# Attention: the new rows' projection with high and low parts in one 40-column stationary

## The chip, the cores and the metric

The kernel runs on one core of a Trainium2 chip. The metric is the device time of one execution in microseconds (us). The core has five engines that run their own instruction streams in order and meet through semaphores: TensorE (PE in the profile, PEld for its weight loads), VectorE (DVE), ScalarE (ACT), GpSimd (POOL) and SyncE (SP), which issues most DMAs.

## The reference

Two layers of a decoder are computed for 1024 prompt rows and 8 new ("sample") rows that share every weight. The change touches layer 0's attention, and in it the projection of the 8 new rows:

```
def attn_project(x, w_qkv):
    qkv = x @ w_qkv                      # x: 8 x 1024, w_qkv: 1024 x 1536
    q, k, v = split into 16 q heads, 4 k heads, 4 v heads of 64

def swa_sample(x, k_buf, v_buf, w_qkv, sinks, w_o):
    q, k, v = attn_project(x, w_qkv)
    q, k = rope(q, pos), rope(k, pos)    # rotary positions
    o = sink_attention(q, cache + k, cache + v)
    return o @ w_o, ...
```

All arrays are float32. The kernel multiplies in the format fp32r and splits every operand into a high and a low part (x = xh + xl, w = wh + wl, low = value - high); a product is the sum of xh*wh, xh*wl and xl*wh.

## The kernel before, in words

Attention comes first (the first 390 us), in four groups of heads, `attention(g)`, once on each engine. A group has its own weights `wh`, `wl`: three slabs for q and k and v (384 output columns in all) and two for the output projection. The rows go through in nine blocks: b = 0 to 7 are 128 prompt rows each, b = 8 (`NB`) is the 8 new rows.

On TensorE, `project(b)` multiplies a block: for each of 8 contraction tiles of 128, three products (`accumulate`, L677 to L679), each with the rows as the stationary operand (128 columns, or 8 for b = 8) and 384 weight columns as the moving one. The result stands in bank 0 or 1 (b % 2). Then a pipeline of steps follows, a few blocks behind: `scores` (L810), `turn` (transposes of q and k, L785, for the new rows L788), `values` (L831), `turn_probs` (L821), and `down`, the output projection (L677 to L679 again, on `a_oh` and `a_ol`). The order is written out by hand. In a turn t of the loop `for t in range(NB + 1)` TensorE runs project(t), scores(t - 2), turn(t - 1), values(t - 4), turn_probs(t - 3). After the loop, in groups 0 to 2, it runs turn(8) and then `down(0, 4)`; in the last group `down(4, 6)` stands in turn 8 before values, and `down(6, 8)` before turn(8). TensorE's `down` of q = 4 in the last group waits for the rotary products of the new rows, since it writes the bank that these read.

Behind project(8) the data go like this. ScalarE copies the values out of the bank (`v_in`, L1361, `a_vs`). VectorE waits for that copy (semaphore `v_fp`), and makes the rotary products (`rope`, L1918 to L1920, `a_t`). GpSimd adds them up (`add_rope`, L2616 and L2621, `a_qk`), and TensorE turns the sum (L788). VectorE's order in a turn t is `inverse(t - 3)` (L1959, L1961), `rope(t)`, `shift(t - 2)` (mask, maximum and sink, L1946 to L1954), `t_lo(t - 1)` (low parts of the turned q and k, L1926 and L1928), `heads_lo(t - 4)` (L1967). TensorE's turn(b) waits for `a_qk` of block b and for t_lo(b - 1), since it overwrites the bank that t_lo reads. GpSimd also multiplies the probabilities by the inverse sums (`probs`, L2627).

The steps of `scores`, `shift`, `t_hi` and `t_lo` run over prompt blocks only, apart from t_lo(8), a copy (L1933).

Of the kernel before, what the change touches and what calls it, by code (L numbers as in the profile page):

```python
# [6 lines left out]
F32 = mybir.dt.float32  # L7
F32R = mybir.dt.float32r
ALU = mybir.AluOpType
# [3 lines left out]
P = 128  # L13
D = 1024
SEQ = 1024
NS = 8
TOK = SEQ + NS
KT = D // P
# [6 lines left out]
NB = SEQ // W  # L25
# [104 lines left out]
J = {key: n + 1 for n, key in enumerate(JOBS)}  # L130
# [229 lines left out]
def fillers():  # L360
# [10 lines left out]
    for n in range(NB):  # L371
# [13 lines left out]
        "p_in prod rot plain out_r0 out_r1 out_p0 out_p1").split()  # L385
ATT_SEMS = ("table_in turn_in cache_in rope_t v_in v_fp qk back t_hi t_lo score shifted small small2 expd "
            "inv probs pt pt_in heads heads_hi heads_lo kv_out win_out s_sc s_scc "
            "s_tr s_mx s_ex s_p s_pt s_ptc s_o s_of s_oh s_ol dchain").split()
RET_SEMS = ("m_in dec_in cq0 cq1 cv cg0 cg1 turned q_hi q_lo v_hi v_lo k_hi k_lo inner inn i_hi i_lo kv state out_ "
            "s_hi s_lo stats small root ga back ob ob_hi ob_lo oh_out ol_out st_in0 st_in1 st_out0 st_out1 decay outer "  # L390
            "x_in x_ing masks rows x_part x_sum xv xv_out vb x_o x_stats x_small x_root x_ga x_back xo xo_hi xo_lo xoh_out xol_out "
# [3 lines left out]
def after(eng, sem, value):  # L395

    if value > 0:
        eng.wait_ge(sem, value)
# [39 lines left out]
def build(nc, A):  # L438
    ctx = ExitStack()
    with ctx:  # L440
        K = Kit()
# [8 lines left out]
        def place(at):  # L450

            here = [at]

            def sb(name, shape, dt=F32):
                size = 4 * math.prod(shape[1:])
                t = nc.alloc_sbuf_tensor_at(name, shape, dt, offset=here[0], align_bytes=32)
                here[0] += (size + 31) // 32 * 32
                assert here[0] <= TOP, (name, here[0])
                return t
            return sb  # L460

        sb = place(BASE)
# [16 lines left out]
        sb = place(REGION)  # L479
# [10 lines left out]
        sb = place(at_t2 + 32 * TH)  # L490
        K.t2r = sb("x_t2r", [P, 2, 4, TH])
        sb = place(at_t2 + 80 * TH)
        K.t1r = sb("x_t1r", [P, 4, TH])
        sb = place(at_t2)
        K.ha = (sb("h_ah", [P, 4, TOK], F32R), sb("h_al", [P, 4, TOK], F32R))
        K.h0 = (sb("h_0h", [P, BATCH, TOK], F32R), sb("h_0l", [P, BATCH, TOK], F32R))
        sb = place(REGION + 49568)
        K.ms = sb("n_ms", [P, CH])
        K.sq = sb("n_sq", [P, KT, CH])
        sb = place(REGION)  # L500
        K.lsq = sb("n_lsq", [P, KT, CH])
        sb = place(REGION)
        K.hs = sb("h_in", [P, 2, 4, CH])
        at_x = BASE + 4 * SLAB * (RAW + 12)
        sb = place(at_x + 4 * KT * TOK)
        K.xr = sb("x_r", [P, 4, TOK])
        sb = place(at_x)
# [4 lines left out]
        for i in range(2):  # L512
            sb = place(BASE + 4 * SLAB * (RAW + 6 * i + 4))
# [3 lines left out]
        sb = place(REGION)  # L517
# [23 lines left out]
        K.same = sb("same", [32, NS])  # L541
        K.a_t1 = sb("a_t1", [P, 2, 320])
        K.a_t2 = sb("a_t2", [P, 2, 320])
        sb("a_gap", [P, 1536])
        K.a_sm = sb("a_sm", [P, GH, 2 * W])
        K.a_qh = sb("a_qh", [P, 256], F32R)
        K.a_ql = sb("a_ql", [P, 256], F32R)
# [5 lines left out]
        sb = place(REGION)  # L553
# [36 lines left out]
        sb = place(BASE + 4 * SLAB * (RAW + 4))  # L590
# [3 lines left out]
        sb = place(BASE + 4 * SLAB * (RAW + 6 + 4))  # L594
# [31 lines left out]
def wait_slab(eng, S, s):  # L626

    wait_unit(eng, S, UNIT_OF_SLAB[s])
# [54 lines left out]
def tensor_engine(pe, K):  # L683
    S, T, R, bank = K.S, K.T, K.R, K.bank
    wh, wl, xh, xl, ident = K.wh, K.wl, K.xh, K.xl, K.ident
# [61 lines left out]
    def attention(g):  # L747
# [8 lines left out]
        def project(b):  # L756
            m = P if b < NB else NS
            if b == 0:
                wait_slab(pe, S, 5 * g + 2)
            if b < 2 and g:  # L760
                pe.wait_ge(*freed(g, b))
            if g == 0:
                pe.wait_ge(S["x_lo"], 1 + sum((b + 1) * W > end for _, end in PIECES[:-1]))
            if b >= 2:
                pe.wait_ge(T["rope_t"], (NB + 1) * g + b - 1)
            if last and b == NB:
                pe.wait_ge(S["yadd"], 24 * g + 3)
            o = bank[b % 2][0:m, 0:384].rearrange("m (a n) -> m a n", a=3)
            t = slice(b * W, b * W + m)
            terms = []  # L770
            for k in range(KT):
                kk = slice(k * P, (k + 1) * P)
                terms.append((xh[:, k, t], xl[:, k, t], wh[:, 0:3, kk], wl[:, 0:3, kk]))
            accumulate(pe, o, terms).then_inc(S["jobs"], 1)
# [473 lines left out]
def scalar_engine(act, K):  # L1248
    A, S, T, R, bank = K.A, K.S, K.T, K.R, K.bank
    xh, y = K.xh, K.y  # L1250
# [97 lines left out]
    def attention(g):  # L1348
        last = g == NG - 1

        def v_in(b):
            act.wait_ge(S["jobs"], J["qkv", g, b])
            if b < NB:
                after(act, T["heads"], NB * g + max(b - 4, 0))
                act.activation(K.a_v[:, b % VR, :], bank[b % 2][:, 320:384], ACT.Copy).then_inc(T["v_in"], 1)
            if b == NB - 1:
                after(act, T["kv_out"], 64 * g)
                act.activation(K.a_vf[:, :], bank[b % 2][:, 320:384], ACT.Copy).then_inc(T["v_fp"], 1)
            if b == NB:
                after(act, T["s_o"], g)  # L1360
                act.activation(K.a_vs[:, :], bank[b % 2][0:NS, 320:384], ACT.Copy).then_inc(T["v_fp"], 1)  # L1361

        def t_hi(b):
# [451 lines left out]
def vector_engine(dve, K):  # L1815
    S, T, R, bank = K.S, K.T, K.R, K.bank
    xh, xl, y, ident = K.xh, K.xl, K.y, K.ident
    split = [0]

    def split_lo(n):  # L1820

        dve.wait_ge(S["hi_done"], n + 1)
        source, (hi, lo) = unit_source(K, n), unit_hi_lo(K, n)
        if n >= U_LAST:
            i = n - U_LAST
            dve.scalar_tensor_tensor(lo, source, K.wm[:, i:i + 1], hi.bitcast(F32), ALU.add, ALU.subtract).then_inc(S["lo_done"], 1)
            return
        dve.tensor_tensor(lo, source, hi.bitcast(F32), ALU.subtract).then_inc(S["lo_done"], 1)  # L1828
# [74 lines left out]
    def attention(g):  # L1903
        last = g == NG - 1

        def rope(b):
            m = P if b < NB else NS
            if b < NB:
                dve.wait_ge(T["v_in"], NB * g + b + 1)
            if b >= NB - 1:  # L1910
                dve.wait_ge(T["v_fp"], 2 * g + b - NB + 2)
            after(dve, T["qk"], 2 * (NB + 1) * g + (2 * (b - 1) if b >= 2 else 0))
            src = bank[b % 2][0:m, 0:320].rearrange("m (h a n) -> m h a n", h=5, a=2)
            a1 = K.a_t1[0:m, b % 2, :].rearrange("m (h a n) -> m h a n", h=5, a=2)
            a2 = K.a_t2[0:m, b % 2, :].rearrange("m (h a n) -> m h a n", h=5, a=2)
            cs = K.cosT[0:m, b:b + 1, :].rearrange("m (a c) n -> m a c n", a=1)
            sn = K.sinT[0:m, b, :].rearrange("m (a n) -> m a n", a=1)
            dve.tensor_tensor(a1, src, cs.to_broadcast([m, 5, 2, 32]), ALU.mult)  # L1918
            dve.tensor_tensor(a2[:, :, 1, :], src[:, :, 0, :], sn.to_broadcast([m, 5, 32]), ALU.mult)
            dve.scalar_tensor_tensor(a2[:, :, 0, :], src[:, :, 1, :], -1.0, sn.to_broadcast([m, 5, 32]),  # L1920
                                     ALU.mult, ALU.mult).then_inc(T["rope_t"], 1)
# [101 lines left out]
        def add_y(q0, q1):  # L2023
            for q in range(q0, q1):
                add(("ao", g, q))

        for t in range(NB + 1):
            if t >= 3:
                inverse(t - 3)
            rope(t)  # L2030
            if t >= 2:
                shift(t - 2)
            if t >= 1:
                t_lo(t - 1)
            if g == 0 and t < 2:
                x_lo(2 + t)
            if g == 0 and t in (4, 5):
                split_lo(t - 1)
            if last and t == NB:
                add_y(4, 6)  # L2040
            if t >= 4:
                heads_lo(t - 4)
            if last and t == NB - 1:
                add_y(0, 4)
# [1156 lines left out]
```

## Time and profile before

| | us |
|---|---|
| median of 3 runs | 2746.16 |
| shortest and longest run | 2745.92 and 2748.1 |
| the profiled execution: its span, first to last instruction | 2744.9 |
| TensorE busy in it | 2692.8 |
| VectorE busy in it | 1638.9 |
| ScalarE busy in it | 1036.3 |

Of the profiled execution only its span is given; the median of the runs lies 1.3 us above it, for what lies before the first and after the last instruction and the spread of the runs. TensorE is busy in 98% of the span, so most of the time is its products one after another; where it waits shows in its timeline as idle time, with the instruction that ended the wait.

### The profile page before, as it was taken

To read this page: it belongs to the slowest core of one execution; us is meant where nothing else is said; L and a number is where in the kernel's file an instruction comes from. 1 tells how busy PE (TensorE), PEld (TensorE's weight loads), DVE (VectorE), ACT (ScalarE), POOL (GpSimd) and SP (SyncE) were. 2 spreads that over 40 slices of the span, in tenths; PEclk is the share of its full clock that TensorE was granted. 3 is DMA by queue.
4 is the path that set the end of the run, shared out by engine and by line. 5 is a ranking of instruction groups with operands and counts; after the bars stand their busy time and mean duration, and the time that the engine had idled before them with its cause. 6 is when DMAs were issued, how large, how long until landed. Compare 5 with 4: busy or idle time off the path is not lost.

```text
span 2744.9 us, 47495 instructions
## 1 busy us (share of the span) xinstructions
PE 2692.8 (98%) x19166; PEld 2587.3 (94%) x19166; DVE 1638.9 (60%) x3042; ACT 1036.3 (38%) x1930; POOL 673.5 (25%) x534
## 2 busy tenths in 40 slices
PE   8999989999999999999999999999999999999997
PEld 7888879999999999999999999999999999999997
DVE  6556578676767445615446354366688666766455
ACT  5445455433343112323343433432254344332123
POOL 2344351322220002403213122111241223220021
PEclk9999999999999999999999999999999999999999
DMA  4210111222224232235666565686512222223321
GB/s 141 82 44 15 40 33 55 70 86 78 86 78 154 74 112 68 79 111 166 184 197 189 184 194 186 204 267 215 171 55 73 79 84 71 86 96 123 114 73 62
DMA packets 218665, 307.27 MB, mean 112 GB/s; under 512 B 30608, under 2 KB 171536, under 8 KB 218416
## 3 DMA queue, kind: packets, MB, share of 16 engines
q1 hardware_dynamic: 153552, 242.73, 28.0%
q10 hardware_dynamic: 64896, 61.50, 6.6%
q8 instruction: 153, 2.51, 0.4%
q14 instruction: 64, 0.52, 0.1%
HBM read 214.81 MB, written 91.45 MB: 112 GB/s over the span
## 4 chain that ended last, share of the span: by engine, by line
PE 91%; DVE 4%; ACT 2%; issue 1%; POOL 1%; DMA 0%; ACTq 0%; SPq 0%; POOLq 0%; DVEq 0%
PE bank L677 19%; PE bank L679 19%; PE bank L678 18%; PE bank L970 9%; PE bank L972 9%; PE bank L971 9%; PE bank L831 1%; PE bank L810 1%; PE bank L1201 1%; PE bank L1154 1%; PE bank L1163 1%; PE bank L821 1%; PE bank L785 0%; PE bank L1148 0%; DVE y L1866 0%
## 5 line engine op out<-in xcount | busy, mean ns | idle before, releaser
L1828 DVE TENSOR_TENSOR wl<-raw,wh 128x512 fp32r<-128x512 f32 (+1 forms) x381 | 367.6, 971 | 362.8 <-ACT wh L1269 358.4
L677 PE MATMUL bank<-xh,wh 128*128 128x344 f32 x1616 | 525.5, 325 | 1.5 <-DVE f_cv L2135 1.5
L679 PE MATMUL bank<-xh,wl 128*128 128x344 f32 x1616 | 516.8, 320 | 0.0
L678 PE MATMUL bank<-xl,wh 128*128 128x344 f32 x1616 | 516.0, 319 | 0.0
L1269 ACT ACTIVATE wh<-raw 128x512 fp32r<-128x512 f32 (+1 forms) x412 | 307.8, 764 | 367.0 <-PE bank L679 231.0
L970 PE MATMUL bank<-xh,wh 128*128 128x258 f32 x1280 | 362.0, 283 | 0.0
L972 PE MATMUL bank<-xh,wl 128*128 128x258 f32 x1280 | 361.6, 282 | 0.0
L971 PE MATMUL bank<-xl,wh 128*128 128x258 f32 x1280 | 361.1, 282 | 0.0
L1856 DVE TENSOR_TENSOR y<-bank,y 128x344 f32<-128x344 f32 x384 | 192.1, 512 | 231.5 <-PE bank L679 230.7
L677 PEld LDWEIGHTS bank<-xh,wh 128*128 128x128 f32 x1616 | 304.1, 188 | 16.1 <-issue 9.1
L678 PEld LDWEIGHTS bank<-xl,wh 128*128 128x128 f32 x1616 | 303.8, 188 | 4.7
L679 PEld LDWEIGHTS bank<-xh,wl 128*128 128x128 f32 x1616 | 304.0, 188 | 0.0
L971 PEld LDWEIGHTS bank<-xl,wh 128*128 128x128 f32 x1280 | 242.0, 189 | 0.0
L970 PEld LDWEIGHTS bank<-xh,wh 128*128 128x128 f32 x1280 | 241.6, 189 | 0.0
L972 PEld LDWEIGHTS bank<-xh,wl 128*128 128x128 f32 x1280 | 241.4, 189 | 0.0
L2684 POOL TENSOR_TENSOR raw<-raw 128x512 f32<-128x512 f32 x40 | 51.5, 1288 | 589.0 <-DVE wl L1828 588.9
L970 PE MATMUL bank<-x_t2h,wh 128*128 128x258 f32 x640 | 181.0, 283 | 2.0 <-ACT f_ab L1487 2.0
L971 PE MATMUL bank<-x_t2l,wh 128*128 128x258 f32 x640 | 180.9, 283 | 0.0
L972 PE MATMUL bank<-x_t2h,wl 128*128 128x258 f32 x640 | 180.5, 282 | 0.0
L677 PE MATMUL bank<-h_ah,wh 128*128 128x344 f32 x480 | 154.4, 322 | 0.0
L679 PE MATMUL bank<-h_ah,wl 128*128 128x344 f32 x480 | 153.9, 321 | 0.0
L678 PE MATMUL bank<-h_al,wh 128*128 128x344 f32 x480 | 153.3, 319 | 0.0
(294 smaller groups left out, 6202.5 us busy)
## 6 DMA issues: line engine op xcount, KB each, us to landing
raw<-in_w SPq DMA_DIRECT2D x216, 512.0 KB, 3.8
scratch_h<-f_g SPq DMA_DIRECT2D x40, 516.0 KB, 2.7
h_in<-scratch_h SPq DMA_DIRECT2D x30, 688.0 KB, 5.1
scratch_qkvg<-p_plain ACTq DMA_DIRECT2D x96, 172.0 KB, 2.9
r_s<-in_state_in SPq DMA_DIRECT2D x32, 512.0 KB, 3.8
out_state_s<-r_s ACTq DMA_DIRECT2D x32, 512.0 KB, 5.1
scratch_qkvg<-p_rot ACTq DMA_DIRECT2D x24, 344.0 KB, 2.9
xh<-scratch_heads_hi SPq DMA_DIRECT2D x12, 688.0 KB, 8.1
```

The source lines that it names most:

```text
L677: pe.matmul(out, ah, bh, start=(k == 0), stop=False)
L678: pe.matmul(out, ah, bl, start=False, stop=False)
L679: mm = pe.matmul(out, al, bh, start=False, stop=(k == n - 1))
L810: mm = pe.matmul(out, qs[r, q], keys, start=(n_pass == 0), stop=(n_pass == 2))
L821: mm = pe.transpose(bank[5 + half][:, at:at + HD], K.a_prob[r, b % 2, h, t * W:(t + 1) * W], ident[r, r])
L970: pe.matmul(out, hi[:, kk], bh, start=(k == 0 and not adds), stop=False, skip_group_check=adds)
L971: pe.matmul(out, hi[:, kk], bl, start=False, stop=False, skip_group_check=adds)
L972: mm = pe.matmul(out, lo[:, kk], bh, start=False, stop=(k == 3), skip_group_check=adds)
L1269: act.activation(hi, source, ACT.Copy).then_inc(S["hi_done"], 1)
L1828: dve.tensor_tensor(lo, source, hi.bitcast(F32), ALU.subtract).then_inc(S["lo_done"], 1)
L1856: dve.tensor_tensor(t, bank[b][:, 0:CH], t, ALU.add).then_inc(S["yadd"], 1)
L2684: pool.tensor_tensor(g[:, two], g[:, one], g[:, two], ALU.add).then_inc(S["w_sum"], 1)
```

## The change

For the block of new rows alone, TensorE's stationary is a new tile `a_two` of 40 columns for each contraction tile: columns 0 to 7 hold the rows' high parts, 8 to 31 are zero, 32 to 39 hold the low parts. Two products, with `wh` and with `wl`, take the place of the three. The bank then has the sum with the high parts in partitions 0 to 7 and the sum with the low parts in 32 to 39 (the product of both low parts, formerly left out, is now in it). VectorE copies partitions 32 to 39 to `a_low`, waits for its own copy, and adds it onto partitions 0 to 7 of the bank, before the rotary products of this block. In the diff the parts follow one another: the tiles, TensorE's `project`, ScalarE's `v_in`, VectorE's `rope` and VectorE's loop over turns. ScalarE's copy of the values waits for that addition. The stationary is built once, on VectorE in turn 3 of group 0. Both new tiles lie in a gap of SBUF that was left free; no other tile moves.

```
+        K.a_two = sb("a_two", [P, KT, 40], F32R)
+        K.a_low = sb("a_low", [NS, 384])
-        sb("a_gap", [P, 1536])
+        sb("a_gap", [P, 1536 - 704])
...
+            if b == NB:
+                pe.wait_ge(T["two"], 2)
+                both = bank[b % 2][0:40, 0:384].rearrange("m (a n) -> m a n", a=3)
+                for k in range(KT):
+                    kk = slice(k * P, (k + 1) * P)
+                    pe.matmul(both, K.a_two[:, k, :], wh[:, 0:3, kk], start=(k == 0), stop=False)
+                    mm = pe.matmul(both, K.a_two[:, k, :], wl[:, 0:3, kk], start=False, stop=(k == KT - 1))
+                mm.then_inc(S["jobs"], 1)
+                return
...
             if b == NB:
                 after(act, T["s_o"], g)
+                act.wait_ge(T["joined"], 2 * g + 2)
                 act.activation(K.a_vs[:, :], bank[b % 2][0:NS, 320:384], ACT.Copy).then_inc(T["v_fp"], 1)
...
+            if b == NB:
+                dve.wait_ge(S["jobs"], J["qkv", g, b])
+                dve.tensor_copy(K.a_low[:, :], bank[b % 2][32:32 + NS, 0:384]).then_inc(T["joined"], 1)
+                dve.wait_ge(T["joined"], 2 * g + 1)
+                dve.tensor_tensor(bank[b % 2][0:NS, 0:384], bank[b % 2][0:NS, 0:384], K.a_low[:, :], ALU.add).then_inc(T["joined"], 1)
             if b >= NB - 1:
                 dve.wait_ge(T["v_fp"], 2 * g + b - NB + 2)
...
+            if g == 0 and t == 3:
+                dve.memset(K.a_two[:, :, NS:32].bitcast(F32), 0.0)
+                dve.tensor_copy(K.a_two[:, :, 0:NS], xh[:, :, SEQ:TOK].bitcast(F32)).then_inc(T["two"], 1)
+                dve.tensor_copy(K.a_two[:, :, 32:32 + NS], xl[:, :, SEQ:TOK].bitcast(F32)).then_inc(T["two"], 1)
```

VectorE's stream in group 0, turn 8, before: the end of inverse(5), then the rotary products of the new rows, and the first of shift(6).

```order
L1959 TENSOR_TENSOR a_st<-a_st 128x4
L1961 RECIPROCAL a_st<-a_st 128x4
L1918 TENSOR_TENSOR a_t_114<-bank,cosT 8x320
L1919 TENSOR_TENSOR a_t_115<-bank,sinT 8x5x32
L1920 SCALAR_TENSOR_TENSOR a_t_115<-bank,sinT 8x5x32
L1946 ISA a_sm,a_st<-bank,mask 128x256
```

The same place in the changed kernel (its lines are numbered 17 higher here).

```order
L1976 TENSOR_TENSOR a_st<-a_st 128x4
L1978 RECIPROCAL a_st<-a_st 128x4
L1924 COPY a_low<-bank 8x384
L1926 TENSOR_TENSOR bank<-bank,a_low 8x384
L1935 TENSOR_TENSOR a_t_114<-bank,cosT 8x320
L1936 TENSOR_TENSOR a_t_115<-bank,sinT 8x5x32
L1937 SCALAR_TENSOR_TENSOR a_t_115<-bank,sinT 8x5x32
L1963 ISA a_sm,a_st<-bank,mask 128x256
```

The copy and the addition stand between inverse(5) and the rotary products; all that follows is in the old order.

TensorE's stream at the same place, before: the last contraction tile of the new rows' block, scores(6), turn(7), values(4), turn_probs(5), then turn(8) and the first output product.

```order
L677 MATMUL bank<-wh,xh 8x384
L678 MATMUL bank<-wl,xh 8x384
L679 MATMUL bank<-wh,xl 8x384
L810 MATMUL bank<-a_kh,a_qh 128x256 x2
...
L810 MATMUL bank<-a_kh,a_ql 128x256 x2
L785 MATMUL bank<-ident,a_qk 128x128 x3
L831 MATMUL bank<-a_pt,a_v 64x256 x4
L821 MATMUL bank<-ident,a_prob 128x64 x16
L788 MATMUL bank<-ident,a_qk 64x8 x5
L677 MATMUL bank<-a_oh,wh 128x344
```

The same place in the changed kernel.

```order
L777 MATMUL bank<-wh,a_two 40x384
L778 MATMUL bank<-wl,a_two 40x384
L821 MATMUL bank<-a_kh,a_qh 128x256 x2
...
L821 MATMUL bank<-a_kh,a_ql 128x256 x2
L796 MATMUL bank<-ident,a_qk 128x128 x3
L842 MATMUL bank<-a_pt,a_v 64x256 x4
L832 MATMUL bank<-ident,a_prob 128x64 x16
L799 MATMUL bank<-ident,a_qk 64x8 x5
L679 MATMUL bank<-a_oh,wh 128x344
```

The block has two products a contraction tile in place of three; nothing behind it has moved.

## Rows read from the trace of the kernel before

**Rows 1.** The head of the page: span, busy time and share of an engine, instructions.

```profile
span 2744.9 us, 47495 instructions
PE 2692.8 (98%) x19166; PEld 2587.3 (94%) x19166; DVE 1638.9 (60%) x3042; ACT 1036.3 (38%) x1930; POOL 673.5 (25%) x534
```

**Rows 2.** TensorE's groups by shape, 0 to 400 us: xcount | busy, mean ns.

```profile
L677 PE MATMUL bank<-wh,xh 128*128 128x384 f32 x256 | 89.8, 351 | 11.9 <-DVE wl L1828 11.9
...
L677 PE MATMUL bank<-wh,xh 128*8 128x384 f32 x32 | 10.8, 336 | 0.0
```

**Rows 3.** Timeline, group 0, TensorE: start, duration, instruction, [idle before <-releaser].

```profile
65.37 0.34 PE L677 MATMUL bank<-wh,xh 128*8 128x384 f32 x1
...
69.37 0.33 PE L679 MATMUL bank<-wh,xl 128*8 128x384 f32 x1
...
72.03 0.71 PE L821 MATMUL bank<-ident,a_prob 64*128 64x64 f32 x16
...
73.44 0.30 PE L788 MATMUL bank<-ident,a_qk 8*64 8x8 f32 x5 [0.70 <-DVE a_kl L1928]
```

**Rows 4.** TensorE's waits, 0 to 370 us: total, times, longest.

```profile
PE bank L788 <- DVE a_kl L1928: 2.1, 3, 0.7
```

**Rows 5.** Busy time (and instructions) of each engine in two stretches, groups 0, 2.

```profile
65.00:70.00 5.00, 5.00 (x45) 2.69 (x42) 2.22 (x12) 4.08 (x14) 1.69 (x2) 1.00 0.00 0
...
247.00:252.00 5.00, 5.00 (x45) 2.70 (x42) 2.23 (x11) 4.10 (x14) 1.69 (x2) 1.00 0.00 0
```

**Rows 6.** Timeline, group 0, ScalarE, VectorE and GpSimd.

```profile
67.89 1.08 ACT L1386 ACTIVATE a_pt<-bank 128x512 f32<-128x512 f32 x2
...
68.35 1.89 POOL L2627 TENSOR_TENSOR a_prob<-a_prob,a_st 128x1024 f32<-128x1024 f32 x1 [3.31 <-DVE a_st L1961]
...
69.74 0.21 ACT L1361 ACTIVATE a_vs<-bank 8x64 f32<-8x64 f32 x1 [0.77 <-PE bank L679]
...
69.98 0.48 DVE L1918 TENSOR_TENSOR a_t<-bank,cosT 8x320 f32<-8x320 f32 x1 [1.72 <-ACT a_vs L1361]
...
72.33 0.16 DVE L1951 TENSOR_TENSOR a_st<-a_st,sinkb 128x4 f32<-128x4 f32 x1
...
73.01 0.28 DVE L1928 TENSOR_TENSOR a_kl<-bank,a_kh 128x128 fp32r<-128x128 f32 x1
```

**Rows 7.** VectorE's groups by shape, 0 to 400 us: xcount | busy, mean ns.

```profile
L1878 DVE RECIPROCAL bank<-bank 128x344 f32<-128x344 f32 x1 | 2.3, 2316 | 0.2 <-ACT bank L1301 0.2
...
L1918 DVE TENSOR_TENSOR a_t<-bank,cosT 8x320 f32<-8x320 f32 x4 | 1.9, 480 | 8.8 <-ACT a_vs L1361 8.8
L1933 DVE COPY a_sq<-bank 64x40 f32<-64x40 f32 x8 | 1.5, 190 | 0.1
...
L1919 DVE TENSOR_TENSOR a_t<-bank,sinT 8x160 f32<-8x160 f32 x4 | 1.2, 302 | 0.0
```

**Rows 8.** Timeline, last group, the engines together.

```profile
343.65 1.89 POOL L2627 TENSOR_TENSOR a_prob<-a_prob,a_st 128x1024 f32<-128x1024 f32 x1 [5.58 <-DVE a_st L1961]
...
347.82 0.30 DVE L1920 SCALAR_TENSOR_TENSOR a_t<-bank,sinT 8x160 f32<-8x160 f32 x1
...
348.18 0.43 PE L677 MATMUL bank<-a_oh,wh 128*128 128x344 f32 x1
...
349.32 0.91 POOL L2665 TENSOR_TENSOR n_ms<-y 128x344 f32<-128x344 f32 x1
...
349.53 0.72 DVE L1951 TENSOR_TENSOR a_st<-a_st,sinkb 128x4 f32<-128x4 f32 x1
...
354.88 1.89 POOL L2627 TENSOR_TENSOR a_prob<-a_prob,a_st 128x1024 f32<-128x1024 f32 x1 [0.37 <-DVE a_st L1961]
...
355.69 0.39 DVE L1933 COPY a_sq<-bank 64x40 f32<-64x40 f32 x2
```

**Rows 9.** Timeline, group 0, turn 4, VectorE: the end of an idle time.

```profile
39.62 0.16 DVE L1959 TENSOR_TENSOR a_st<-a_st 128x4 f32<-128x4 f32 x1 [1.71 <-ACT a_st L1378]
```

**Rows 10.** A stretch after the last group: busy PE, PEld, DVE, ACT, POOL, then PEclk.

```profile
379.50:386.30 6.80, 4.91 (x17) 4.94 (x18) 4.79 (x10) 5.51 (x8) 3.25 (x4) 0.50 0.26 89
```

More of the change, by code:

```diff
@@ L387 @@
             "inv probs pt pt_in heads heads_hi heads_lo kv_out win_out s_sc s_scc "
-            "s_tr s_mx s_ex s_p s_pt s_ptc s_o s_of s_oh s_ol dchain").split()
+            "two joined s_tr s_mx s_ex s_p s_pt s_ptc s_o s_of s_oh s_ol dchain").split()
 RET_SEMS = ("m_in dec_in cq0 cq1 cv cg0 cg1 turned q_hi q_lo v_hi v_lo k_hi k_lo inner inn i_hi i_lo kv state out_ "
```

## The prediction

> **What bounds the kernel now.** I read the page's head first. TensorE is busy 98% of 2744.9 us [rows 1], so removed products are worth their full time unless something behind them waits for another engine. All that the diff touches lies in the attention stage, so the second view is the table of TensorE's groups there by shape: the new rows' block has 3 x 32 products whose stationary is 8 columns wide, 336 ns each, against 351 ns for one of 128 columns [rows 2]. Third, TensorE's timeline around that block in the first group. The 24 products start at 65.37 and the last one at 69.37, so they stand 4.00 / 23 = 0.174 us apart; the last ends at 69.70. Behind them come the scores, transposes and probability products of older blocks, the last of them (L821) from 72.03 to 72.74, and then TensorE stands still for 0.70 us until 73.44, where it turns the new rows' own q and k (L788) [rows 3]. The reader is to see here that TensorE is not the bound at that point: something else ends last. The table of waits says what: L788 waited three times for VectorE's a_kl (L1928), 0.7 us each [rows 4], in groups 0 to 2. Busy times of the five us around the block are the same in groups 0 and 2 [rows 5], so one group may be worked out for all three.
>
> The fourth view is the same stretch on the other engines [rows 6]. ScalarE copies the new rows' values (L1361) at 69.74, 0.04 us after the block's end; it ends at 69.95, and 0.03 us later VectorE begins the rotary products of the new rows at 69.98, having stood idle for 1.72 us. From there VectorE works without a pause, rotary, then the mask and maximum of block 6 (L1946 to L1954), then L1928, which ends at 73.29. That is 3.31 us in order on one engine, and TensorE's L788 starts 0.15 us after it. So in groups 0 to 2 the end of this stretch is set by **when VectorE may begin the rotary products**, not by how soon TensorE is through.
>
> **What it removes.** Eight of 24 products per group: 8 x 0.174 = 1.39 us, 5.57 us in four groups, 0.20% of the time. A 40-column stationary is between the 8 and the 128 columns whose products differ by 15 ns [rows 2], and both kinds are hidden behind the same moving operand, so I take 0.174 us for the new products too. The block then ends at 68.31 in place of 69.70.
>
> **What it adds in each group.** On VectorE, ahead of the rotary products, a copy of 8x384 numbers out of the bank, a wait for it, and an addition of 8x384 back into the bank; ScalarE's copy of the values waits for that addition, and the rotary products wait for ScalarE as before. The prices come from the groups of VectorE's instructions [rows 7]: 8x320 out of a bank takes 480 ns, 8x160 takes 302, so 1.11 ns an element over a fixed 0.12 us, and 384 elements take 0.55 us. I take 0.55 for the copy and 0.55 for the addition. From below the copy is bounded by the copy of 40 elements, 0.19 us, the addition by the 0.48 us of 320 elements. From above, the only VectorE row that writes a bank is the reciprocal, 2.32 us for 344 elements; it is another operation, and the tensor-tensor rows are nearer, so it counts for the tail only. Each hand-over costs the 0.03 us seen from ScalarE to VectorE.
>
> **Where this lies.** VectorE has idled for 1.72 us before 69.98 [rows 6], so it is free from 68.26 on and the new work goes into that idle time, but it is on the path to the rotary products. In group 0: block ends 68.31, copy 68.35 to 68.90, addition 68.93 to 69.48, ScalarE 69.51 to 69.72 (it is free: L1386 ends at 68.97, [rows 6]), rotary from 69.75 in place of 69.98. The gain that is left is 1.39 - 0.55 - 0.55 - 0.06 = **0.23 us**. Queued behind on VectorE are L1946 to L1928, and TensorE's L788 waits for the last of them; the products L677 that follow stand behind L788 in TensorE's queue. TensorE comes to L788 1.39 us sooner and leaves 0.23 us sooner: its wait grows from 0.70 to 1.86 us. With the bounds of the two prices the gain is 0.66 us at best.
>
> **The last group** has another order: two output products' tiles stand between the transposes and L788, and the first of them (L677 at 348.18) may only start when the rotary products have freed its bank. They ended at 348.12 [rows 8], so that wait is just covered today and no more. When TensorE comes 1.39 us sooner, at 346.79, the rotary products end 0.23 us sooner, at 347.89, and a wait of 1.1 us opens there. What follows there hangs on the same chain. So again 0.23 us.
>
> **Once, in group 0's fourth turn,** VectorE builds the stationary: a fill of 128x192 and two copies of 128x64, by the same slope 0.33 + 2 x 0.19 = 0.7 us. They stand behind L1928 of that turn, where VectorE then sits idle for 1.71 us until ScalarE's exponentials [rows 9]: they cost nothing; without that cover, 0.7 us once. They are done some 26 us before the first use, so TensorE's wait for them is free.
>
> **Sum.** 4 x 0.23 = 0.9 us off the profiled execution, whose span is 2744.9 us; the median of the runs is 2746.16, 1.3 us above the span for what lies around it, which the change does not touch. 2746.16 - 0.92 = **2745.2 us**.
>
> **A rule that speaks against it.** While the new copy would run, GpSimd multiplies the probabilities (L2627, 68.35 to 70.24, [rows 6]) in groups 0 to 2. VectorE can be held by that engine: in the last group L1951, whose two inputs lie in SBUF, took 0.72 us from 349.53 and ended with GpSimd's L2665 at 350.23 [rows 8], against 0.16 us at 72.33 [rows 6]. But the rotary product at 69.98, which reads a bank and one SBUF table, began while GpSimd still multiplied and took its usual 0.48 us [rows 6, 7]. The new addition reads a bank and one SBUF tile and is of this kind. Copies out of a bank were not held either: the two of L1933 at 355.69 took 0.39 us together, 0.19 each as ever [rows 7], within GpSimd's L2627 of 354.88 to 356.77 [rows 8]; they are 40 elements long, not 384. The Trainium skill ("SBUF — State Buffer", Who interferes with whom) says that a VectorE copy may run in a mode that locks the port pair shared with GpSimd, the one who comes second being fully blocked; its page "VectorE: DVE Perf Modes" (Why PSUM operands drop a tier) says that a PSUM operand rules that mode out. By the first alone the copy would wait for GpSimd (rival 2), by the second it runs at 0.55 us.
>
> **The rivals.**
> 1. The full gain reaches the end, 5.57 us, 2740.6 us. It needs L788 and the last group's L677 not to hang on VectorE's chain. Against it: three waits of 0.7 us on exactly this chain.
> 2. Slower: GpSimd holds the copy. In groups 0 to 2 it would start at 70.24 instead of 68.35, 1.89 us later, so each loses 1.66 us; in the last group L2627 ends at 345.54 [rows 8], before the copy at 345.55. 3 x 1.66 - 0.23 = 4.8 us more, 2750.9 us. It turns from gain to loss when the copy is held by over 0.23 us. For it: L1951's 0.72 us; against it: the 0.48 us at 69.98 and L1933.
> 3. Slower: writing a bank makes the addition as dear as the reciprocal, 2.32 us. Each group loses 2.32 - 0.55 - 0.23 = 1.54 us, 6.2 us in all, 2752.3 us.
> 4. The change does not do what it says: sixteen products with 40 columns take as long as the 24 of 8 columns. Then the join's 1.16 us is added four times, 4.6 us, 2750.8 us. Against it: 336 and 351 ns on both sides.
> 5. The clock. Behind the idle stretches of the last group TensorE was granted half its clock (1.2 in place of 2.4 GHz) from 379.5 to 386.3, with 4.91 us of products in it [rows 10]; at full clock these take half, so the stretch is worth at most 2.5 us. Other waits ahead of it may take it away (2742.8 us) or, as waits grow to 1.86 us elsewhere, bring a second one (2747.7 us). In groups 0 to 2 the 0.70 us waits brought none.
>
> **How the numbers follow.** Forecast 0.72; full gain 0.04; held copy 0.05; dear addition 0.03; dear products 0.03; clock 0.10, half on each side; something else 0.03. The range goes from 2742.8 (clock stretch gone; the cheapest prices of the join give 2743.5) to 2748.5 (a second stretch, and the runs of before lie up to 1.9 us above their median): it holds the forecast and the clock cases, 0.82. It leaves out both rivals of a whole gain and the held copy. A measurement of this kernel can tell about 0.2%, 5.5 us, from no change. Faster by more than that is only the full gain, 0.03; slower by more the dear addition and a rest, 0.04; within it 0.93.
>
> **What would show it.** Right: sixteen products 0.174 us apart; copy and addition at about 0.55 us each; L788's wait at 1.86 us in three groups; a new wait of 1.1 us for the rotary products in the last group; the span at 2744.0. Wrong: a copy that ends with GpSimd's multiplication (rival 2); an addition far above 0.6 us (3); products more than 0.18 us apart (4); L788 without a longer wait (1); another length of the half-clock stretch (5).

## The result, and the profile after

| | before | after |
|---|---|---|
| median of 21 runs each, same chip | 2746.57 us | 2750.48 us |
| lowest to highest | 2745.42 to 2748.10 us | 2748.28 to 2751.71 us |
| the profiled execution | 2744.9 us of span | 2751.57 us, 2749.8 us of span |
| mean granted TensorE clock of the profiled execution | 0.997 | 0.994 |

The ratio is 1.0014, with an interval of 1.0007 to 1.0020: slower by 3.9 us, and less than the 0.2% that was set as "no change". The forecast of 2745.2 us and its range, up to 2748.5, lie below it. Lines of the code have moved: L788 of before is now L799 and waits for a_kl L1945; L677, L678 and L679 are L679, L680 and L681; the eight rows' products are L777 and L778.

**The work itself became smaller.** The head of the page of after, the answer to [rows 1], and the new products among TensorE's groups by shape (0 to 400 us; count | busy, mean ns), the answer to [rows 2]:

```profile
span 2749.8 us, 47445 instructions
PE 2693.1 (98%) x19134; PEld 2591.5 (94%) x19134; DVE 1645.2 (60%) x3053; ACT 1035.5 (38%) x1930; POOL 672.3 (24%) x534
...
L777 PE MATMUL bank<-wh,a_two 128*40 128x384 f32 x32 | 10.9, 340 | 0.0
L778 PE MATMUL bank<-wl,a_two 128*40 128x384 f32 x32 | 10.7, 335 | 0.0
```

There are 32 products fewer, each of the new ones lasts 335 or 340 ns as the old did, and yet TensorE is busy for 0.3 us more than before. So other products must have become longer.

**Around the new rows' block nearly all goes as forecast.** Timelines of group 0 of after, of GpSimd, VectorE, ScalarE and TensorE (start, duration, instruction, idle time before and its releaser), the answers to [rows 6] and [rows 3]:

```profile
67.09 1.89 POOL L2648 TENSOR_TENSOR a_prob<-a_prob,a_st 128x1024 f32<-128x1024 f32 x1 [3.31 <-DVE a_st L1978]
...
67.12 0.55 DVE L1924 COPY a_low<-bank 8x384 f32<-8x384 f32 x1
67.70 0.55 DVE L1926 TENSOR_TENSOR bank<-bank,a_low 8x384 f32<-8x384 f32 x1
68.59 0.48 DVE L1935 TENSOR_TENSOR a_t<-bank,cosT 8x320 f32<-8x320 f32 x1 [0.34 <-ACT a_vs L1373]
...
71.62 0.28 DVE L1945 TENSOR_TENSOR a_kl<-bank,a_kh 128x128 fp32r<-128x128 f32 x1
...
68.35 0.21 ACT L1373 ACTIVATE a_vs<-bank 8x64 f32<-8x64 f32 x1 [0.63 <-DVE bank L1926]
```

```profile
64.11 0.37 PE L777 MATMUL bank<-wh,a_two 128*40 128x384 f32 x1
...
66.74 0.34 PE L778 MATMUL bank<-wl,a_two 128*40 128x384 f32 x1
...
72.05 0.29 PE L799 MATMUL bank<-ident,a_qk 8*64 8x8 f32 x5 [1.93 <-DVE a_kl L1945]
72.28 0.43 PE L679 MATMUL bank<-a_oh,wh 128*128 128x344 f32 x1
...
73.93 0.49 PE L679 MATMUL bank<-a_oh,wh 128*128 128x344 f32 x1
74.21 0.49 PE L680 MATMUL bank<-a_ol,wh 128*128 128x344 f32 x1
74.50 0.49 PE L681 MATMUL bank<-a_oh,wl 128*128 128x344 f32 x1
...
77.07 0.32 PE L681 MATMUL bank<-a_oh,wl 128*128 128x344 f32 x1
77.23 0.31 PE L679 MATMUL bank<-a_oh,wh 128*128 128x344 f32 x1
...
77.54 0.32 PE L681 MATMUL bank<-a_oh,wl 128*128 128x344 f32 x1
...
396.20 0.32 PE L681 MATMUL bank<-a_oh,wl 128*128 128x344 f32 x1
```

From the block's start to L799 it is 72.05 - 64.11 = 7.94 us; from the block to L788 it was 73.44 - 65.37 = 8.07 us [rows 3]. So group 0 gains 0.13 us there (groups 1 and 2 gain 0.10 and 0.13). What stands behind it loses ten times as much: the 24 output products start at 72.28 and the last of them at 77.54, 5.26 us; in before the first and the last of the same 24, and the last output product of the attention, are

```profile
73.67 0.43 PE L677 MATMUL bank<-a_oh,wh 128*128 128x344 f32 x1
...
77.40 0.32 PE L679 MATMUL bank<-a_oh,wl 128*128 128x344 f32 x1
...
391.69 0.32 PE L679 MATMUL bank<-a_oh,wl 128*128 128x344 f32 x1
```

The 24 take 3.73 us. That is 1.53 us more for the same products. The table by stretches says why (busy time of PE, PEld, DVE, ACT and POOL with instructions, then the granted clock, DMA share, GB/s). First after, four stretches; then before, the stretch of 73.60:

```profile
73.60:77.10 3.50, 3.50 (x15) 3.50 (x14) 1.55 (x5) 1.09 (x2) 1.20 (x1) 0.51 0.00 0
165.80:169.20 3.40, 3.40 (x13) 3.40 (x13) 1.28 (x4) 1.32 (x5) 0.60 (x1) 0.50 0.00 0
257.90:261.40 3.50, 3.50 (x14) 3.50 (x14) 1.36 (x5) 1.64 (x5) 0.17 (x1) 0.51 0.02 5
367.10:370.60 3.50, 3.42 (x12) 3.42 (x13) 1.47 (x9) 3.14 (x3) 2.77 (x2) 0.51 0.00 0
```

```profile
73.60:77.10 3.50, 3.50 (x27) 3.48 (x25) 2.40 (x9) 2.60 (x9) 0.35 (x1) 1.00 0.02 5
```

TensorE is busy throughout both, but in after at half its clock (1.2 in place of 2.4 GHz): 15 products in 3.5 us where before had 27. There are four such stretches that before does not have, besides the one of 6.8 us that both have after the last group [rows 10] and one at the very end that both have too. Three lie just behind L799, where the wait has grown. The fourth lies in the last group, behind a wait of 0.96 us for y that before has too, some 16 us after the wait of 1.1 us that the change opens; that this new wait brought it is not shown. TensorE's waits of after, 0 to 400 us (total, times, longest), the answer to [rows 4]:

```profile
PE bank L799 <- DVE a_kl L1945: 5.8, 3, 2.0
...
PE bank L679 <- DVE a_t L1937: 1.1, 1, 1.1
```

**The account of the profiled execution.** TensorE reached the block of group 0 already 1.26 us sooner than in before (64.11; 65.37 [rows 3]), and the change has no part in that. Its first wait was 0.6 us shorter (11.3 us; 11.9 us before [rows 2]), and its first products, 0.32 us apart in both, came to 0.17 us apart from 15.6 on, in before only from 17.7 on; in all the profiles of this document this moment lies between 15.6 and 18.0. From that block to the last output product of the attention it is 396.20 - 64.11 = 332.09 us, and 391.69 - 65.37 = 326.32 us in before: 5.8 us more. Four stretches at 1.5 us are 6.1 us; less 0.5 us of gain in four groups, with 0.2 us more in the stretch behind the last group, that is the sum. Behind the attention this execution lost another 0.4 us, so the span is 4.9 us longer.

**Not every run has four.** A stretch of 3.41 us at half clock lowers the mean granted clock of the whole by 0.5 x 3.41 / 2750 = 0.0006, so the mean clock of a run, which each run has, tells roughly how many there were. The profiled executions of all the kernels below bear this out: 0.997 goes with none of these stretches, 0.996 with one or two, 0.995 with three, 0.994 with four. The 21 runs of after stand at 0.994 (8 runs, mean 2751.4 us), 0.995 (7, 2750.2 us) and 0.996 (6, 2749.0 us). Before stands at 0.997 in 59 of 81 runs beside the experiments (2745.9 us) and at 0.996 in 22 (2747.3 us). The fewer, the faster, in both kernels.

### The profile page after: what moved, and what is told of

Read it like the earlier page. It is cut to its first block, busy times and chain, and to the rows that moved or that the text cites. A ratio compares the mean times of both kernels' runs of the same rounds, so it can differ in the third digit from the quotient of the medians.

```text
span 2749.8 us, 47445 instructions
## 1 busy us (share of the span) xinstructions
PE 2693.1 (98%) x19134; PEld 2591.5 (94%) x19134; DVE 1645.2 (60%) x3053; ACT 1035.5 (38%) x1930; POOL 672.3 (24%) x534
## 4 chain that ended last, share of the span: by engine, by line
PE 89%; DVE 5%; issue 2%; ACT 2%; POOL 1%; DMA 1%; SPq 0%; ACTq 0%; POOLq 0%; DVEq 0%
PE bank L679 19%; PE bank L681 18%; PE bank L680 18%; PE bank L981 9%; PE bank L983 9%; PE bank L982 9%; PE bank L842 1%; PE bank L821 1%; PE bank L1212 1%; PE bank L1165 1%; PE bank L1174 1%; DVE wl L1840 1%; PE bank L832 1%; PE bank L1159 0%; PE bank L796 0%
## 5 line engine op out<-in xcount | busy, mean ns | idle before, releaser
L679 PE MATMUL bank<-xh,wh 128*128 128x344 f32 x1616 | 524.9, 325 | 1.5 <-DVE f_cv L2156 1.5
L681 PE MATMUL bank<-xh,wl 128*128 128x344 f32 x1616 | 516.2, 319 | 0.0
L680 PE MATMUL bank<-xl,wh 128*128 128x344 f32 x1616 | 515.3, 319 | 0.0
L679 PEld LDWEIGHTS bank<-xh,wh 128*128 128x128 f32 x1616 | 303.8, 188 | 16.2 <-issue 9.1
L680 PEld LDWEIGHTS bank<-xl,wh 128*128 128x128 f32 x1616 | 303.5, 188 | 4.7
L681 PEld LDWEIGHTS bank<-xh,wl 128*128 128x128 f32 x1616 | 303.6, 188 | 0.0
L679 PE MATMUL bank<-h_ah,wh 128*128 128x344 f32 x480 | 154.2, 321 | 0.0
L681 PE MATMUL bank<-h_ah,wl 128*128 128x344 f32 x480 | 153.7, 320 | 0.0
L680 PE MATMUL bank<-h_al,wh 128*128 128x344 f32 x480 | 153.1, 319 | 0.0
```

Source lines behind the costliest of these rows:

```text
L679: pe.matmul(out, ah, bh, start=(k == 0), stop=False)
L680: pe.matmul(out, ah, bl, start=False, stop=False)
L681: mm = pe.matmul(out, al, bh, start=False, stop=(k == n - 1))
```

## The experiments

All were timed against before on the same chip, whose median was 2746.25 us for fill8, no_join, late_join and swap, 2746.35 us for fill4, after_pad, late_pad and before_swap, and 2745.69 us for swap_g and swap_gf; beside after it was 2746.57 us. Because it differs by up to 0.9 us, two kernels of different sets are compared here by how far each lies from its own before. Two theories stood at the start: that the half-clock stretches follow from the grown waits of TensorE, and the rival that something else of the change costs the time (the addition into the bank, or the new block's form).

**fill8: fill the wait with products that nobody reads.** The wait for a_kl becomes short, and all else is as in after.

```
+        def spin(n):
+            ...
+            for i in range(n):
+                pe.matmul(bank[1][0:40, 0:384], K.a_two[:, i, :], xh[:, i, 0:384], start=(i == 0), stop=(i == n - 1))
...
+                spin(6)
                 down(4, 6)
...
+        spin(8)
         turn(NB)
```

> The changed kernel with products of no use in TensorE's longer wait: eight of them (stationary a_two, 384 moving columns, into bank 1, which nobody reads then) between turn_probs(5) and turn(8) in groups 0 to 2, six before the output tile q = 4 in the last group. VectorE's chain is untouched, so no transfer or step should end sooner or later. Theory (the wait of 1.93 us lets the granted clock fall to half for 3.41 us of the products behind it): the waits shrink to 1.93 - 8 x 0.174 = 0.54 us, no half-clock stretch follows them, 2746.6 - 0.9 = 2745.7 us. Rival (the half clock comes from the block's new products, 16 of 40 columns in place of 24 of 8, and not from the wait): the stretches stay, 2750.5 us.

Measured: 2744.57 us (11 runs, 2743.48 to 2745.96), ratio to before 0.9995 (0.9986 to 1.0004). This is after with 30 products more, and it is 5.6 us faster than after (1.7 us below its before, after 3.9 us above). TensorE's timeline in group 0, then the stretch behind it:

```profile
71.01 1.59 PE L906 MATMUL bank<-xh,a_two 128*40 128x384 f32 x8
73.01 0.29 PE L799 MATMUL bank<-ident,a_qk 8*64 8x8 f32 x5 [0.41 <-DVE a_kl L1955]
...
73.00:77.00 4.00, 3.99 (x29) 3.98 (x29) 2.79 (x9) 2.63 (x9) 0.69 (x1) 1.00 0.01 4
```

L799 starts 7.94 us after the block's start at 65.07, as in after, with 0.41 us of wait left, and the products behind it run at full clock. 10 of 11 runs have a mean clock of 0.997. The copy, the addition and the block are all in this kernel, so the rival falls: the time went into the clock, and the clock followed from the idle time of TensorE.

**fill4: half of it** (`spin(4)` in groups 0 to 2, `spin(3)` in the last).

> As fill8, with four products of no use in place of eight in the wait of groups 0 to 2, and three in place of six in the last group: the wait is about 1.93 - 0.70 = 1.2 us, nothing ends sooner or later. Theory (it is the length of the wait that brings the half clock; a wait of 1.16 us brought none in the kernel without the join): no stretch behind these waits, as fill8, 2744.6 us. Rival (any wait above the 0.70 us of before does it in some runs): between fill8 and the changed kernel, 2746 to 2750 us, with a lower mean clock than 0.997 in most runs.

Measured: 2745.51 us (11 runs, 2744.78 to 2747.11), ratio 0.9999 (0.9990 to 1.0008); 2744.6 us was expected.

```profile
PE bank L799 <- DVE a_kl L1955: 3.4, 3, 1.1
...
PE bank L679 <- DVE a_t L1947: 0.6, 1, 0.6
```

With waits of 1.1 us no stretch beyond the common one stands in the profile; 8 of 11 runs have a mean clock of 0.997, 3 have 0.996, much the same shares as in before. So the stretches behind L799 fall away somewhere between 1.1 and 1.9 us of wait.

**no_join: the shorter block without copy and addition.** The low parts' products are left out of the new rows' projection, and ScalarE waits for the block alone. It measures the most that the removed products could give if the join cost nothing.

```
-                act.wait_ge(T["joined"], 2 * g + 2)
...
-            if b == NB:
-                dve.wait_ge(S["jobs"], J["qkv", g, b])
-                dve.tensor_copy(K.a_low[:, :], bank[b % 2][32:32 + NS, 0:384]).then_inc(T["joined"], 1)
-                dve.wait_ge(T["joined"], 2 * g + 1)
-                dve.tensor_tensor(bank[b % 2][0:NS, 0:384], bank[b % 2][0:NS, 0:384], K.a_low[:, :], ALU.add).then_inc(T["joined"], 1)
```

> The changed kernel without its join: VectorE neither copies nor adds the low parts and ScalarE doesn't wait for them, so the new rows' projection lacks the products of their low parts. Theory (wait, then clock): the block ends 1.39 us sooner and the rotary products begin 1.39 us sooner, L788's wait is 0.70 us again, no half-clock stretch follows, the whole gain of 4 x 1.39 = 5.6 us arrives, 2741.0 us. Rival (the 40-column products bring the half clock): the stretches stay and take back about 1.5 us in each group, 2747 us.

Measured: 2742.55 us (11 runs, 2741.36 to 2743.45), ratio 0.9986 (0.9978 to 0.9995), all runs at 0.997. TensorE's wait and two of ScalarE's instructions in group 0:

```profile
PE bank L799 <- DVE a_kl L1939: 3.5, 3, 1.2
...
67.05 1.09 ACT L1397 ACTIVATE a_pt<-bank 128x512 f32<-128x512 f32 x2
68.02 0.20 ACT L1372 ACTIVATE a_vs<-bank 8x64 f32<-8x64 f32 x1
```

Even a free join does not give the full 1.39 us per group. ScalarE's copy of the values now stands behind L1397 in that engine's queue, which ended in good time before the change; TensorE's wait is 1.2 us in place of 0.70, so 0.46 us of the 1.39 become waiting in groups 0 to 2 and 0.93 us remain; in the last group nothing waits and the whole 1.39 us remains. 3 x 0.93 + 1.39 = 4.2 us, and in the profile the attention from the block of group 0 on is 4.2 us shorter than in before; the medians differ by 3.7 us, where 5.6 us was expected.

**late_join: the old block, with the copy and an addition into an unused tile put ahead of the rotary products.** ScalarE's copy of the values waits for that addition, as in after. It is the join alone, without the shorter block.

```
+            if b == NB:
+                dve.wait_ge(S["jobs"], J["qkv", g, b])
+                dve.tensor_copy(K.a_low[:, :], bank[b % 2][0:NS, 0:384]).then_inc(T["joined"], 1)
+                dve.wait_ge(T["joined"], 2 * g + 1)
+                dve.tensor_tensor(K.a_low2[:, :], bank[b % 2][0:NS, 0:384], K.a_low[:, :], ALU.add).then_inc(T["joined"], 1)
```

> The kernel before with its 24 products of 8 columns, and a copy and an addition of 8x384 ahead of the rotary products as in the changed kernel, but into a tile that nobody reads. Theory (wait, then clock): the rotary products begin 1.17 us later in each group, L788's wait becomes 0.70 + 1.17 = 1.87 us, and half-clock stretches of 3.41 us follow it although the block is the old one: 2746.6 + 4 x 1.17 + 3 or 4 x 1.5 = 2756 to 2757 us. Rival (the new products bring the half clock): the waits alone, 2751.3 us, no stretch.

Measured: 2750.58 us (11 runs, 2748.34 to 2754.16), ratio 1.0017 (1.0008 to 1.0026). Waits, and the stretch behind the first of them, in the profiled execution, which took 2754.16 us:

```profile
PE bank L790 <- DVE a_kl L1936: 5.8, 3, 1.9
...
73.90:77.30 3.40, 3.38 (x16) 3.38 (x17) 1.52 (x5) 2.63 (x9) 0.00 (x0) 0.50 0.02 5
```

The same waits as in after bring such stretches with the old block too, three in this execution: the 40 columns are not needed for it. But the expected 2756 to 2757 us was a miss: 6 of 11 runs stand at 0.997 (mean 2749.7 us), so most runs have fewer stretches than after. In the profile the join adds 3 x 1.2 us to L790's waits and 1.1 us to the last group's, 4.8 us; the runs at 0.997 lie only 3.7 us above those of before (2746.0 us on this chip), and most of the difference of 1.1 us is not explained.

**after_pad and late_pad: the same waits at other distances.** Eight products that nobody reads, 1.39 us, at the end of each of the groups 0 to 2, once on after and once on late_join (there with the 8-column stationary). No wait is changed by it, only when the next one falls.

```
         down(14, 24)
+        pe.wait_ge(T["heads_lo"], NB * (g + 1))
+        for i in range(8):
+            pe.matmul(bank[7][0:40, 0:384], K.a_two[:, i, :], xh[:, i, 0:384], start=(i == 0), stop=(i == 7))
```

> The changed kernel with eight products of no use behind the last output tile of groups 0 to 2 (into bank 7, 1.39 us, no wait): each group is 1.39 us longer, its wait of 1.93 us is the same. In the kernel with 8-column products and a late join, the same wait was followed by half clock in fewer runs. Theory (whether half clock follows a wait of this length hangs on when the wait falls, so another distance from wait to wait changes how many runs have it): the mean clock of the runs is higher than the changed kernel's 0.994 to 0.996, some have 0.997; 2750.5 + 4.2 less up to 3, so 2751.7 to 2753.5 us. Rival (the 40-column block itself makes half clock more likely): the same clocks as the changed kernel, 2754.7 us.

> The kernel before with its old block and a late join, as in late_join, with eight products of no use behind the last output tile of groups 0 to 2 (1.39 us each, no wait). Theory (it hangs on when the wait falls): another mix of mean clocks than late_join's (six of eleven runs at 0.997), the time away from 2750.6 + 4.2 = 2754.8 us by up to 3 us, upward if more runs have the stretches. Rival (the old block makes it rare): the same mix, 2754.8 us.

Measured: after_pad 2751.18 us (11 runs, 2748.14 to 2751.90), ratio 1.0016 (1.0008 to 1.0025), mean clock 0.996 in 8 runs and 0.997 in 3; late_pad 2758.53 us (5 runs, 2756.34 to 2761.20), ratio 1.0047 (1.0034 to 1.0059), mean clock 0.994 to 0.996. In after_pad, groups 0, 1 and 2, with the waits as in after:

```profile
PE bank L799 <- DVE a_kl L1948: 5.8, 3, 2.0
...
73.00:77.00 4.00, 3.98 (x29) 3.98 (x29) 2.79 (x9) 2.65 (x9) 0.66 (x1) 1.00 0.02 4
167.20:170.60 3.40, 3.40 (x14) 3.40 (x13) 1.43 (x5) 0.81 (x2) 1.54 (x1) 0.50 0.00 0
259.30:262.70 3.40, 3.40 (x16) 3.38 (x16) 1.41 (x5) 2.54 (x9) 0.00 (x0) 0.50 0.00 0
```

In late_pad, groups 0 and 2 (group 1 is as group 0, and a third stretch stands in the last group):

```profile
76.00:79.40 3.40, 3.40 (x13) 3.40 (x13) 1.28 (x4) 1.33 (x5) 0.58 (x1) 0.50 0.00 0
...
265.00:269.00 4.00, 3.98 (x29) 3.98 (x29) 2.80 (x9) 2.65 (x9) 0.68 (x1) 1.00 0.00 0
```

The pad adds 3 x 1.39 = 4.2 us of work. To after it cost only 0.9 us, a little less than its theory gave, because stretches went, two of four in the profiles; to late_join it cost 7.9 us, more than its theory allowed, because stretches came. One and the same wait of 1.9 us is followed by half clock in one place and not in another, in either block. after, late_join and the two kernels with pads have twelve waits of 1.9 us for a_kl in their profiles: ten are followed by half clock, which begins 0.0 to 1.8 us after the wait's end, and two are not. The six waits of 1.1 and 1.2 us in fill4 and no_join are followed by none. So the wait makes the stretch possible, and whether it comes changes with when the wait falls. The three runs of after_pad at 0.997 (mean 2749.2 us) less 4.2 us of pad give 2745.0 us: an estimate of what after would take without a stretch.

**swap, before_swap, swap_g and swap_gf: useful work into the wait.** In groups 0 to 2 the first output tile goes to the other bank and ahead of the turn of the new rows, so TensorE has 0.94 us of its own work there; in the last group tile 4 changes its bank, so that tile 5 is the first to need the new rows' bank. swap is on after in all groups, before_swap the same edit on before; swap_g leaves the last group as in after, and swap_gf is swap_g with six products that nobody reads in the last group's wait.

```
-        return q % 2
+        return (q + 1) % 2 if g < NG - 1 or q >= 4 else q % 2
...
+        down(0, 1)
         turn(NB)
-        down(0, 4)
+        down(1, 4)
```

> The changed kernel with useful work in the wait: in groups 0 to 2 the output tile q = 0 (six products, 0.94 us) goes into bank 1 and stands ahead of turn(8), q = 1 takes bank 0; in the last group q = 4 goes into bank 1, so that q = 5 is the first to need the new rows' bank. Theory (wait, then clock): L788's wait falls from 1.93 to about 1.0 us, no half-clock stretch follows, and the 0.94 us are saved behind it: 2746.6 - 0.9 - 3 x 0.94 - 0.9 = 2742.0 us. Rival (the new products bring the half clock): four stretches stay, 2748 us. Should 1.0 us of waiting already bring the half clock, the stretches stay too, but in this kernel and not in fill8.

> The kernel before with the output tile q = 0 in bank 1 ahead of turn(8) in groups 0 to 2, and q = 4 of the last group in bank 1, as in swap, but with the old block of 24 products and no join. TensorE's 0.94 us of products fill the wait of 0.70 us for VectorE: 3 x 0.70 = 2.1 us less, 2744.2 us, no half clock behind L788. If the gain of swap comes from the order alone, this kernel is as fast as swap (2743.7 us); if the 1.39 us of removed products count once the wait is filled, swap stays ahead by up to 1 us a group.

> The changed kernel with q = 0 in bank 1 ahead of turn(8) in groups 0 to 2 alone; the last group is as in the changed kernel, with its wait of 1.15 us ahead of q = 4. In swap and before_swap, whose last group was reordered, a half-clock stretch stood at 367 to 369 us that before does not have. Theory (it came from the last group's reordering): no stretch there, the last group's wait of 1.15 us costs nothing new, 2743.5 us. Rival (the wait of 1.15 us brings it as well, as in the changed kernel's profile, where one stands at 367 us): stretch in some runs, 2745 us.

> As swap_g, with six products of no use ahead of q = 4 in the last group, which fill its wait of 1.15 us. Theory (only waits bring the half clock): no stretch besides the one that before has too, mean clock 0.997 in nearly all runs, 2743.0 us. Rival (the stretch at 367 us belongs to the last group's other waits and comes and goes by where they fall): stretches in some runs here too, 2744 to 2745 us.

| | median us | lowest to highest, 11 runs | ratio to before (interval) | runs at 0.997 / 0.996 |
|---|---|---|---|---|
| swap | 2743.70 | 2742.02 to 2744.80 | 0.9991 (0.9982 to 1.0000) | 6 / 5 |
| before_swap | 2745.18 | 2743.82 to 2746.91 | 0.9996 (0.9987 to 1.0005) | 6 / 5 |
| swap_g | 2745.99 | 2743.87 to 2747.33 | 1.0000 (0.9991 to 1.0009) | 3 / 8 |
| swap_gf | 2744.20 | 2743.27 to 2746.06 | 0.9994 (0.9986 to 1.0003) | 8 / 3 |

swap, group 0, TensorE:

```profile
72.47 0.29 PE L799 MATMUL bank<-ident,a_qk 8*64 8x8 f32 x5 [0.79 <-DVE a_kl L1946]
...
74.12 0.42 PE L679 MATMUL bank<-a_oh,wh 128*128 128x344 f32 x1 [0.22 <-DVE y L1867]
```

The wait for a_kl falls to 0.79 us, no stretch follows it in groups 0 to 2, and swap is 6.5 us faster than after. But 0.22 us of what was gained is lost two tiles later, where the bank has to be emptied by VectorE. The bet of 2742.0 us was 1.7 us too low, in part for that and for a stretch in the last group, which its profile has; 5 of its 11 runs stand at 0.996. before_swap was expected at 2744.2 us. swap lies 1.4 us further below its before than before_swap does, so some of the removed products' time seems to count once the wait is filled, though the two intervals overlap.

swap_g and swap_gf came out as their rivals had it. swap_gf is 1.8 us faster than swap_g and has more runs at 0.997, which would fit a price of the last group's 1.1 us wait. But the two intervals overlap, and the profiles speak against it. That wait stands in those of after, late_join, after_pad, late_pad and swap_g, and none has half clock in the 16 us behind it; swap_g's own has no new stretch at all. And in the profiled execution of swap_gf, its slowest run (2746.06 us), half clock stands in the last group although that wait was filled; before_swap and swap have one there too. In all three the stretch stands behind a wait of 1.90 us for y, which every version has, before too. swap_gf, then before_swap, then before, which ran at full clock behind it:

```profile
368.25 0.42 PE L679 MATMUL bank<-a_oh,wh 128*128 128x344 f32 x1 [1.90 <-DVE y L1872]
...
368.60:372.00 3.40, 3.40 (x10) 2.26 (x8) 2.28 (x7) 0.00 (x0) 1.51 (x2) 0.50 0.00 0
```

```profile
368.57 0.60 PE L677 MATMUL bank<-a_oh,wh 128*128 128x344 f32 x1 [1.90 <-DVE y L1857]
368.98 0.49 PE L678 MATMUL bank<-a_ol,wh 128*128 128x344 f32 x1
```

```profile
370.45 0.43 PE L677 MATMUL bank<-a_oh,wh 128*128 128x344 f32 x1 [1.90 <-DVE y L1856]
...
370.00:375.00 5.00, 4.55 (x27) 3.24 (x27) 4.66 (x9) 2.76 (x5) 2.40 (x3) 1.00 0.00 0
```

A wait of one length, for one releaser, with half clock behind it or without: this is what the two pads showed, in rows that the change does not touch. Of the twelve profiles, which all have this wait, four have half clock behind it: swap, before_swap, swap_gf and late_pad. after's fourth stretch stands behind another of these waits for y, of 0.96 us. So the last group's stretch comes and goes with when these waits fall; the change's share in it is not shown. None of the four versions is faster than before beyond its interval; swap comes to its edge.

## Why the prediction was wrong

**What held.** The view of what bounds the stretch held in each piece. The copy took 0.55 us and the addition 0.55 us, as sized. Rival 2 fell: both ran while GpSimd multiplied (67.09 to 68.98). The Trainium skill's page "VectorE: DVE Perf Modes" (Why PSUM operands drop a tier) says that an operand in PSUM keeps an instruction out of the mode that needs both SBUF read ports; the copy, not held here, agrees. Rival 3 fell: writing the bank did not make the addition dear. Rival 4 fell: the sixteen products start from 64.11 to 66.74, 0.175 us apart. Rival 1 fell: L799's wait grew, to 1.93 us (1.86 forecast), and the last group's is 1.1 us as forecast. The one error here is small: ScalarE starts 0.10 us after the addition's end (67.70 + 0.55 = 68.25 to 68.35), where 0.03 us was taken. With 0.03 us more in the block, 0.13 us of gain are left of 0.23.

**What failed** is the step from the grown wait to the time: the sum put the cost of a longer wait at nothing and left it to rival 5, whose size and chance were wrong. The prediction saw that waits of 1.86 us might bring half clock and priced it as "a second one", 2.5 us, 2747.7 us, with a chance of 0.05. Its ground was that the 0.70 us waits of before brought none. Two things were wrong in that:

- The price was taken once, though the change makes the same wait three times. The profiled execution has four new stretches, each 1.5 us: three behind the waits of 1.9 us, and one in the last group behind a wait that before has too. Four times are 6.1 us, and with 0.13 us of gain a group the forecast of that case would have been 6.1 - 0.5 = 5.6 us above before.
- The chance was drawn from one profiled execution and from waits of another length. That 0.70 us does no harm was true, and 1.1 us does hardly any in groups 0 to 2 (fill4, no_join); 1.9 us is another matter (after, late_join). The trace of before would even have misled further: its own wait of 1.90 us, at 370.45, was followed by full clock. That was one execution, and four of the other eleven profiles show the other outcome behind the same wait. One row without half clock could not make the case unlikely.

**The rest of the working holds, but its number came out partly by luck.** In the profile of fill8, which has no new stretch, the attention from the block of group 0 to the last output product takes 391.00 - 65.07 = 325.93 us, 0.4 us less than in before: about the 0.5 us of four gains, not the 0.9 us of the forecast. The 2745.0 us of after_pad without its pad lies within 0.2 us of the forecast all the same, in part because some 0.3 us were gained outside the span, which the sum took as untouched: the 81 runs of before last 2.1 to 2.3 us longer than their spans, the 21 of after 1.8 to 1.9 us. Why is not known. fill8's 1.7 us under its before are more than both together, but its interval, 0.9986 to 1.0004, is wide enough for either. The mechanism "the saving turns into waiting" was right; that the waiting itself has a price, in the products behind it, was missed.

**What stays open.** Why one run of after has four stretches and the next one, by its clock, one or two isn't settled. after_pad and late_pad show that the moment of the wait matters; the runs of one kernel differ by themselves. Which moments are bad was not mapped. The Trainium skill ("TensorE: Matmul & The Clock Gate", What's actually happening) says that the chip's watch over TensorE "doesn't reset when your kernel starts", by which one kernel can come out differently from run to run; the spread of the mean clock, 0.994 to 0.996 within after, agrees. Other places for the new rows' block in TensorE's order, or another bank for their turn, were not tried.

## What to carry to other kernels

When products are taken away ahead of a point where TensorE waits for another engine, the saving becomes a longer wait, and that wait can cost half clock in the products behind it: in the profiles here in none of six places at 1.1 to 1.2 us in groups 0 to 2, in ten of twelve at 1.9 us, and then 1.5 us for each place. Price it once for each wait that grows, expect that a wait which the change only moves can gain or lose such a stretch, and don't take one trace without such a stretch for a proof that the next run has none. If a wait must grow, move useful work into it, and read the granted clock behind it beside TensorE's busy share, which looks full at half clock too.

## What the runs showed of the hardware

- At half clock the 344-column products are 0.29 us apart in place of 0.16 us, and TensorE's busy time shows nothing of it: 3.50 of 3.50 us either way.
- It doesn't begin with the wait's end: in group 1 of after L799 ended its wait at 164.51, and the clock fell at about 165.8, after six output products at full clock. In group 0 of late_join it fell within 0.02 us of the wait's end.
- Useless work made a kernel faster: 30 products more (5.2 us by their spacing) took 5.6 us off the median's distance to before.
- Before, too, has runs with an extra stretch: 22 of 81 runs stand at 0.996, 1.5 us slower in the mean than the 59 at 0.997, which is the price of one stretch. No profile of such a run is on record, so where it lies is not shown.
